# Summing three groups of the modulation product on VectorE instead of TensorE

## What is computed

```python
sc, scc = jax.nn.silu(c), jax.nn.silu(c_ctx)
mod_l = sc @ ada_w[i] + ada_b[i]                     # 6 * 1024 values: sh1, s1, g1, sh2, s2, g2
mod_c = scc @ ada_w[i] + ada_b[i]
h = x * (1 + s1) + sh1
x = layernorm(ALPHA * x + g1 * mixer(h), ln1_g[i], ln1_b[i])
x = layernorm(ALPHA * x + g2 * mlp(x * (1 + s2) + sh2), ln2_g[i], ln2_b[i])
```

## Time and profile before

| what | value |
|---|---|
| median of 3 runs | 1933.3 us (1932.83 to 1934.34) |
| the profiled execution's own time | 1933.96 us |
| its span in the profile | 1932.1 us |
| TensorE matmuls busy | 1921.8 us, 99% |
| VectorE busy | 1371.3 us, 71% |
| ScalarE busy | 674.7 us, 35% |
| GpSimd busy | 381.2 us, 20% |
| mean granted TensorE clock | 0.999 |

### The profile page before, as it was taken

The page is one execution under the profiler, slowest core; times in us unless marked ns, Lnnn a source line. Parts: engine busy times, 40 slices in busy tenths (PEclk is TensorE's granted clock), DMA queues, the critical chain, the costliest instruction groups (busy, mean ns, idle before and its releaser), DMA issues.

```text
span 1932.1 us, 24878 instructions
## 1 busy us (share of the span) xinstructions
PE 1921.8 (99%) x9432; PEld 1653.0 (86%) x9432; DVE 1371.3 (71%) x1977; ACT 674.7 (35%) x936; POOL 381.2 (20%) x364
## 2 busy tenths in 40 slices
PE   9999999999999999999999999999999999999998
PEld 6889899899889988998888888888888888888887
DVE  3756587698887777767887755754764787777778
ACT  2423122145323222331546225324413443434443
POOL 0300312313211222222310130130030037110004
PEclk9999999999999999999999999999999999999999
DMA  9623334345998998898596285366447525977656
GB/s 327 262 70 67 120 121 131 106 135 134 210 230 216 215 230 231 229 236 226 175 223 240 88 251 181 129 192 197 151 144 231 173 90 178 246 210 194 175 146 148
DMA packets 120419, 350.59 MB, mean 181 GB/s; under 512 B 17520, under 2 KB 30448, under 8 KB 115568
## 3 DMA queue, kind: packets, MB, share of 16 engines
q1 hardware_dynamic: 91200, 268.11, 40.9%
q0 software_dynamic: 27280, 77.08, 22.2%
q10 hardware_dynamic: 1824, 3.85, 0.6%
HBM read 296.01 MB, written 40.92 MB: 174 GB/s over the span
## 4 chain that ended last, share of the span: by engine, by line
PE 95%; POOL 1%; DMA 1%; DVE 1%; issue 1%; ACT 0%; SPq 0%; POOLq 0%; DVEq 0%; ACTq 0%
PE bank L1157 18%; PE bank L1159 18%; PE bank L1158 18%; PE bank L1195 4%; PE bank L1196 4%; PE bank L1197 4%; PE bank L1565 3%; PE bank L1564 3%; PE bank L1562 3%; PE bank L1626 3%; PE bank L1627 3%; PE bank L1624 3%; PE bank L1809 2%; PE bank L1808 2%; PE bank L1806 2%; PE bank L1468 1%
## 5 line engine op out<-in xcount | busy, mean ns | idle before, releaser
L2377 DVE TENSOR_TENSOR w_lo<-raw,w_hi 128x1024 fp32r<-128x1024 f32 x132 | 168.8, 1282 | 170.8 <-ACT w_hi L1832 170.6
L1832 ACT ACTIVATE w_hi<-raw 128x1024 fp32r<-128x1024 f32 x132 | 139.2, 1055 | 279.3 <-PE bank L1159 158.9
L1157 PE MATMUL bank<-w_hi,act_hi 128*128 128x512 f32 x504 | 198.2, 393 | 0.0
L1159 PE MATMUL bank<-w_hi,act_lo 128*128 128x512 f32 x504 | 196.4, 390 | 0.0
L1158 PE MATMUL bank<-w_lo,act_hi 128*128 128x512 f32 x504 | 196.3, 390 | 0.0
L1157 PE MATMUL bank<-hT_hi,w_hi 128*128 128x384 f32 (+2 forms) x544 | 191.8, 353 | 0.0
L1158 PE MATMUL bank<-hT_lo,w_hi 128*128 128x384 f32 (+2 forms) x544 | 190.8, 351 | 0.0
L1159 PE MATMUL bank<-hT_hi,w_lo 128*128 128x384 f32 (+2 forms) x544 | 190.8, 351 | 0.0
L1195 PE MATMUL bank<-w_hi,hT_hi 128*128 128x512 f32 x336 | 131.0, 390 | 0.0
L1196 PE MATMUL bank<-w_lo,hT_hi 128*128 128x512 f32 x336 | 130.8, 389 | 0.0
L1197 PE MATMUL bank<-w_hi,hT_lo 128*128 128x512 f32 x336 | 130.7, 389 | 0.0
(11 more groups left out here) (458 smaller groups left out, 4858.2 us busy)
## 6 DMA issues: line engine op xcount, KB each, us to landing
raw<-w_units_d SPq DMA_DIRECT2D x234, 512.0 KB, 4.6
mod<-mod_units_d SPq DMA_DIRECT2D x64, 384.0 KB, 4.5
wsum<-w_units_d SPq DMA_DIRECT2D x44, 512.0 KB, 4.5
raw<-weight_sums_d SPq DMA_DIRECT2D x32, 512.0 KB, 4.4
wsum<-w_units_d POOLq DMA_DIRECT2D x25, 512.0 KB, 7.9
wsum<-wsum POOLq DMA_DIRECT2D x19, 512.0 KB, 7.0
bv<-mod_units_d SPq DMA_DIRECT2D x16, 512.0 KB, 3.6
weight_sums_d<-w_units_d POOLq DMA_DIRECT2D x8, 1024.0 KB, 12.4
```

The source lines that it names most:

```text
L1157: nc.tensor.matmul(out, s_hi, m_hi, start=first, stop=False)
L1159: return nc.tensor.matmul(out, s_lo, m_hi, start=False, stop=last)
L1832: nc.scalar.activation(halves_of(phase, k, i)[0], raw[:, s, :], ACT.Copy).then_inc(hi_done, 1)
L2377: tt(lo, raw[:, s, :], f32(hi), ALU.subtract).then_inc(lo_done, 1)
```

## The change

The sum over partitions of the three groups moves to VectorE. It transposes each accumulated tile of 128 x 1024 in blocks of 32 x 32 and sums each block's 32 columns (`part_sum`), which leaves, in each band of 32 partitions, the sums over that band's rows, 32 columns for each vector. Four matmuls (`part_columns`) then add the four bands: the stationary tile `sel32` is 128 x 32, with a one where the partition's number modulo 32 is the column's, and each matmul takes 8 x 2 of the partial sums as moving columns and writes one band of bank 7. VectorE adds the bias (`add_part_bias`). `sel32` is made by one row sum of the identity. The row sums' matmuls, ScalarE's copies and the transposes of the three groups go. In vz VectorE's sums stand between the low halves of units 1 and 2, and the matmuls after unit 2. In the two gmlp trips VectorE's sums stand between the last two low halves of the down stage, the matmuls after token tile 1 of the last sweep, and the bias addition behind the drain of that tile. The semaphore `lg_dve` is renamed `small_done` and also counts `sel32` and the sums. The fourth group, in gmlpz, and the second layer keep the old way.

```diff
@@ order of TensorE's steps
-_VZ = _V[:2] + [("rows2", 6, "A")] + _V[2:3] + [("cols2", 7, "D")] + _V[3:]
+_VZ = _V[:3] + [("cols2", 7, "D")] + _V[3:]
...
-_DOWN0M = _DOWN0[:1] + _ROWS + _COLS + _DOWN0[1:]
+_DOWN0M = _DOWN0[:10] + _COLS + _DOWN0[10:]
@@ buffers and counts
+        part_sums = bst[:, :, :, :].rearrange("p a b c -> p (a b c)")[:, 0:64].rearrange("p (v n) -> p v n", v=2)
+        sel32 = sb("sel32", [P, 32])
...
+        part_sums_v = rbuf[:, 0, 0:64].rearrange("p (v n) -> p v n", v=2)
...
+        def sums_made(phase, i):
+
+            done = 11
+            if phase == "vz":
+                return done
+            return done + 4 * (i + 1)
@@ TensorE
-                            if columns:
-                                columns()
...
-                                    if t == 1 and columns1:
+                                    if t == 1 and half == 1 and columns1:
                                         columns1()
...
-                                if half == 0 and rows:
-                                    rows()
...
+            def part_columns(phase, i, label, n, vectors):
+                sums = part_sums_v if phase == "vz" else part_sums
+
+                pe.wait_ge(small_done, sums_made(phase, i))
+                free(phase, i, label)
+                for q in range(4):
+                    src = sums[:, 0:vectors, 0:4 * n].rearrange("p v (j q) -> p q j v", q=4)[:, q]
+                    last = nc.tensor.matmul(bank[7][32 * q:32 * q + 32, 0:n * vectors].rearrange("p (j v) -> p j v", v=vectors),
+                                            sel32[:, :], src, start=True, stop=True, tile_position=(0, 32 * q))
+                last.then_inc(pe_step, 1)
...
-            def sums_2():
-                pe.wait_ge(mod0_used, KC)
-                mod_sums("vz", 0, "rows2", 6, sums_v, WIDE_M0 // 2)
-
             for phase, i in V_PIECES:
                 token_units(phase, i, 0, "v", TILES0, {} if phase == "v" else {
-                    (1, 5): sums_2, (2, 5): lambda: mod_columns("vz", 0, 2, rbuf[:, 0, :], 7)})
+                    (2, 5): lambda: part_columns(phase, i, "cols2", 8, 2)})
...
                 elif phase != "gmlpz":
-                    down(phase, i, CH, TILES0, act_hi0, act_lo0, ready, rows=rows, columns=columns)
+                    down(phase, i, CH, TILES0, act_hi0, act_lo0, ready,
+                         columns1=lambda: part_columns(phase, i, "cols0", 8, 2))
@@ ScalarE
                 if phase == "vz":
-                    mod_rows(phase, i, 2, rbuf[:, 0, :], 6, step_of("v0", 0, "cols3"))
+                    act.wait_ge(mod0_used, KC)
...
-                    down_splits(phase, i, CH, copy if p else None)
+                    down_splits(phase, i, CH, None)
@@ VectorE
-            def down(phase, i, k0, tiles, then=None):
+            def down(phase, i, k0, tiles, then=None, sums=None, columns=None):
...
                 split_lo(phase, i, k0 + 3)
+                if sums:
+                    sums()
                 if phase == "ffn1a":
                     block_lo(0, 0)
                 else:
                     split_lo(phase, i, k0 + 4)
                 for t in range(tiles):
                     drain(phase, i, 1, t, tiles)
+                    if t == 1 and columns:
+                        columns()
...
+            def part_sum(done, v, a, src, turned, sums=part_sums):
+
+                n = src.shape[1] // 32
+                dve.wait_ge(small_done, done)
+                nc.vector.transpose(turned, src).then_inc(small_done, 1)
+                dve.wait_ge(small_done, done + 1)
+                nc.vector.tensor_reduce(sums[:, v, a:a + n], turned.rearrange("p (n r) -> p n r", r=32),
+                                        mybir.AxisListType.X, ALU.add).then_inc(small_done, 1)
+
+            def add_part_bias(phase, i, label, layer, c, n, vectors):
+
+                dve.wait_ge(pe_step, step_of(phase, i, label))
+                src = bank[7][:, 0:n * vectors].rearrange("p (j v) -> p j v", v=vectors)
+                bias = cols[:, ADAB + 48 * layer + c:ADAB + 48 * layer + c + n].unsqueeze(2).to_broadcast([P, n, 2])
+                tt(modc[:, layer, c:c + n, :], src, bias, ALU.add).then_inc(dve_drain, 1)
...
-                    dve.wait_ge(pe_step, step_of("gmlp", m // KC - 1, "cols0"))
+                    dve.wait_ge(small_done, sums_made("gmlp", m // KC - 1))
...
                 split_lo(phase, i, 1)
                 if n < 2:
                     product_v(4 * n)
+                if n == 2:
+                    dve.wait_ge(mod0_used, KC)
+                    for v in range(2):
+                        part_sum(7 + 2 * v, v, 0, sums_v[v], stage[:, :, :].rearrange("p a b -> p (a b)"), part_sums_v)
                 split_lo(phase, i, 2)
...
+                    nc.vector.tensor_reduce(sel32[:, :], ident[:, :].rearrange("p (x r) -> p r x", x=4), mybir.AxisListType.X,
+                                            ALU.add).then_inc(small_done, 1)
                 split_lo(phase, i, 4)
                 if n < 2:
                     product_v(4 * n + 3)
                 else:
-                    mod0_columns(phase, i, "cols2", 7, 2)
+                    add_part_bias(phase, i, "cols2", 0, 8 * 2, 8, 2)
...
                 if phase != "gmlpz":
-                    def then():
-                        normalise_v(p + 1)
-                        if p:
-                            mod0_columns(phase, i, "cols0", 7, 2 + p)
-                    down(phase, i, CH, TILES0, then)
+                    def group_sums():
+                        dve.wait_ge(mod0_used, KC * (p + 1))
+                        for v in range(2):
+                            part_sum(sums_made(phase, i) - 4 + 2 * v, v, 0, sums_g[v], stage[:, :, :].rearrange("p a b -> p (a b)"))
+
+                    def group_columns():
+                        add_part_bias(phase, i, "cols0", 0, 8 * (2 + p), 8, 2)
+                    if p:
+                        down(phase, i, CH, TILES0, lambda: normalise_v(p + 1), group_sums, group_columns)
+                    else:
+                        down(phase, i, CH, TILES0, lambda: normalise_v(p + 1))
```

More of the change, by code:

```diff
@@ L523, in build @@
         lgh_ready = sem("lgh_ready")
-        lg_dve = sem("lg_dve")
+        small_done = sem("small_done")
         lg_act = sem("lg_act")
@@ L1202, in token_units, with down @@
                             between[q, t]()
-            def down(phase, i, k0, tiles, a_hi, a_lo, ready, late=None, rows=None, columns=None, rows1=None, columns1=None):
+            def down(phase, i, k0, tiles, a_hi, a_lo, ready, late=None, rows1=None, columns1=None):
                 for half in range(2):
@@ L2081, in _ @@
                 if n == 0:
-                    act.wait_ge(lg_dve, 1)
+                    act.wait_ge(small_done, 1)
                     nc.scalar.activation(lg[:, 3, :], lg[:, 2, :], ACT.Ln).then_inc(lg_act, 1)
@@ L2952, in _ @@
                     dve.wait_ge(lg_act, 1)
[L2953 to L2961, removed]
+                    ts(lg[:, 2, :], lg[:, 1, :], -1.0, 1.0, ALU.mult, ALU.add).then_inc(small_done, 1)
+                    dve.wait_ge(small_done, 1)
+                    ts(lg[:, 4, :], lg[:, 2, :], -1.0, 1.0, ALU.mult, ALU.add).then_inc(small_done, 1)
+                    dve.wait_ge(small_done, 2)
+                    ts(lg[:, 4, :], lg[:, 4, :], 1e-30, None, ALU.max).then_inc(small_done, 1)
+                    dve.wait_ge(small_done, 3)
+                    nc.vector.reciprocal(lg[:, 4, :], lg[:, 4, :]).then_inc(small_done, 1)
+                    dve.wait_ge(small_done, 4)
+                    tt(lg[:, 0, :], lg[:, 4, :], lg[:, 1, :], ALU.mult).then_inc(small_done, 1)
                 for t in range(TILES0):
@@ L2968, in _ @@
                 if n == 0:
[L2969 removed]
+                    dve.wait_ge(small_done, 5)
                     dve.wait_ge(lg_act, 2)
[L2971 removed]
+                    tt(lg[:, 0, :], lg[:, 0, :], lg[:, 3, :], ALU.mult).then_inc(small_done, 1)
+                    nc.vector.tensor_reduce(sel32[:, :], ident[:, :].rearrange("p (x r) -> p r x", x=4), mybir.AxisListType.X,
+                                            ALU.add).then_inc(small_done, 1)
                 split_lo(phase, i, 4)
@@ L3199, in _ @@
             dve.wait_ge(dec_in, 32)
-            dve.wait_ge(lg_dve, 6)
+            dve.wait_ge(small_done, 6)
             first_k = first
```

## The result

The changed kernel takes 1946.03 us (median of 6 runs, 1945.14 to 1947.62) against 1933.07 for the kernel before (6 runs): **1.0066 times as long, 95% interval 1.0053 to 1.0079**. It was forecast at 1929.5, at most 1932.9. It came out 13.0 us slower than before and 16.5 us above the forecast. The profiled execution took 1945.8 us, its span 1944.0.

A forecast was written before the change was run, and what follows sets the result against it. TensorE was taken as the bound; 3 x 1.20 (row sums) + 3 x 0.45 (transposes) - 3 x 0.38 (added matmuls) = 3.8 us saved takes the median from 1933.3 to 1929.5 us, range 1928.8 to 1932.9.

The forecast's parts named there:

- What bounds the kernel: Whole kernel: TensorE, busy 99% of the span, so its time removed in the edited places should reach the end.
- Removed 1.65 us a group, added 0.38: TensorE, three groups: row-sum matmuls (1.20 us) and transposes (0.45) go, four narrow matmuls come; net 1.27 us per group.
- The extrapolation over columns: Narrow matmuls: a line through the costs at 512 and 384 columns gives 0.38 us for 16 columns.
- VectorE's instructions at 1.25 us: Two transposes and two row sums per group at 1.25 us each, 5.2 us with waits, between 3.2 and 8.4.
- No stretch beside GpSimd: In gmlp, GpSimd's residual additions would not lengthen the new VectorE instructions; a 0.39 us stretch would use up the spare.
- The room in gmlp, 5.6 us for 5.2: In the edited gmlp down stages VectorE's four instructions fit before TensorE's wait, with 0.4 us to spare.
- The selection matrix is one small row sum: Making sel32 on VectorE takes one small row sum, lying before a 0.80 us wait.
- A: VectorE's transposes pass at half rate; TensorE waits 2.1 us twice in gmlp, giving 1933.7 us; chance 0.13.
- B: The added narrow matmuls cost their full loads, 0.89 us a group, giving 1931.0 us; chance 0.10.
- C: VectorE's transposes and row sums both at half rate; TensorE waits 9.2 us in two pieces; 1938.7 us, slower; chance 0.06.
- D: The time saved on TensorE is lost at the next wait and nothing moves, 1933.3 us; chance 0.04.
- Gaps outside the edited places: The forecast's test: it is wrong if TensorE's gaps grow anywhere outside the named places; no size given.

The follow-up runs named there:

- experiment 2: Changed kernel with sel32 kept in 32 unused columns of layer 1's modulation tile instead of its own tile: 1929.82 us, ratio 0.998.
- experiment 3: Changed kernel with sel32 in the first half of a 256-byte tile instead of a 128-byte one: 1929.49 us, ratio 0.9979.
- experiment 1: Kernel before with an unused tile of 128 bytes a partition where the changed kernel puts sel32: 1949.72 us, ratio 1.0084.
- experiment 8: experiment 2 with each gmlp transpose done twice, the second overwriting the first with the same values: 1934.90 us, ratio 1.0006.
- experiment 6: Kernel before with 128 unused bytes just ahead of w_hi, moving the split weights and all later tiles: 1951.25 us, ratio 1.0092.

## Why the prediction was wrong, point by point

- **What bounds the kernel: right.** TensorE was and is the bound, and its time in the edited places reaches the end: 3 x 1.27 predicted, 3.6 and 3.9 us measured (experiments 2 and 3, where the tiles keep their distances or shift by 256 bytes).
- **Removed 1.65 us a group, added 0.38: right.** The narrow matmuls measured 0.40, the net gain 1.26. The extrapolation over columns was the better choice than the full loads of the earlier trace rows.
- **VectorE's instructions at 1.25 us: right.** Transposes 1.23 to 1.25, row sums 1.22, four of them 5.0 us with their waits. The Trainium skill's "Vector Engine (DVE) Microarchitecture Reference", section 3.8 (one element per cycle per lane), fits: with 1.24 us for 1024 columns the transpose takes as long as the row sum and the two-input instructions of that size, and not twice as long. The figure of "VectorE: DVE Perf Modes", section "The three transpose paths", 311 ns for 128x128 in bf16, would have made it an estimated 2.5; the measurement decides against carrying it over to this fp32 form.
- **No stretch beside GpSimd: right.** GpSimd adds residuals until 288.83 in the changed kernel, over the whole of the first transpose (287.60), which took 1.23 us; the two-input subtraction just ahead of it took 1.62. That agrees with the rule of the Trainium skill's "SBUF — State Buffer", section "Who interferes with whom", that the prediction weighed.
- **The room in gmlp, 5.6 us for 5.2: right, and narrow.** In experiment 2 the last row sum ends at 292.77 + 1.22 = 293.99, and the narrow matmuls are due one spacing after 294.50, at 294.73: 0.7 us to spare. VectorE's slack at gmlpz's first chunk is 0.93 us there (1.04 in the earlier trace rows), so its lag was absorbed.
- **"The selection matrix is one small row sum": the step that failed.** It priced the instruction and left out the tile. The sum 3 x 1.20 + 3 x 0.45 - 3 x 0.38 has no term for it, and gives no reason why placement should cost nothing. The diff's `sb("sel32", [P, 32])` is an edit with a cost of its own: 128 bytes that slide the operands of some 3,400 matmuls against each other, 16.3 us by experiment 1, and 16.2 by the changed kernel against experiment 2. No row of the trace before could price it, which was a reason to name it as unknown and widen the range upward.
- **Rivals A, B and C: none happened.** C had the right sign, from a mechanism that played no part. D is out too, since 3.6 us were gained. None of the four asked what the change does on the side. Their prices rest on "every microsecond that VectorE is late for a TensorE wait costs one", which is too low: in the profile of experiment 8 a wait of 1.73 us cost 3.43.
- **Gaps outside the edited places**: the prediction named them as what would prove it wrong. It was wrong without any gap: TensorE stayed 99% busy and each matmul took longer. The test should have been the spacing of an untouched matmul.

Two versions beat both kernels: experiment 2 (1929.82 us) and experiment 3 (1929.49 us), each by 0.2%, the gain that was forecast. Their intervals overlap; there is nothing to choose between them by time.

## What to carry to other kernels

A new SBUF tile is an edit to every tile that is placed after it. Put it last, or into a tile that exists, or round its size up to a multiple that was measured to be free (256 bytes here, where it restores the cost of the kernel before; no run tells whether another placement would be faster still), and compare the mean duration of untouched matmuls in both profiles before looking for waits. Where TensorE is the bound, a wait on it can cost more than its length: here up to twice, when its clock fell behind it.

## What the runs showed of the hardware that I had not expected

**A shift of a matmul's two operands against each other in a partition changes its spacing.** For products of split fp32 (fp32r) with 512 moving columns and a 128x128 stationary tile, start to start is 0.227 us at the distance of the kernel before, 0.233 at 32 and at 64 bytes from it, 0.232 at 128 and 0.229 at 192 (19 matmuls in a row in a down stage); with 384 columns the mean duration goes from 334 to 338 ns at 128 bytes. A displacement of 256 bytes leaves both unchanged, and moving both operands by 128 bytes does too. Why, stays open. That the moving operand's reads meet the loading of the next matmul's weights is a guess that no run tests, and the exact distances at which the cost begins and ends were not tried.

**A pause of 1.7 to 2.1 us on TensorE was followed by a fall of its clock.** Both pauses in the profile of experiment 8 were followed by about 3 us at 0.43 us a matmul, and the first cost 3.43 us instead of 1.73. TensorE had been busy without a break for over 200 us before it (busy 234.00 us of 234.00 from 56 to 290). The profile of experiment 6 has a third case, in a place that no edit touches, and that of experiment 2 a shorter pause there:
```profile
923.29 0.45 PE L1563 MATMUL bank<-hT_hi,w_hi 128*128 128x384 f32 x1 [2.09 <-DVE w_lo L2509]
```
```profile
913.82 0.44 PE L1577 MATMUL bank<-hT_hi,w_hi 128*128 128x384 f32 x1 [0.91 <-DVE w_lo L2523]
```
After the 2.09 us the granted clock was 1.00 until 924, 0.50 from 925 to 927, and 1.00 again from 928 on. From 920.87 to 928.11 it took 7.24 us for 19 spacings that take 3.33 at 0.1755 each: 3.9 us lost, most of what sets the profiled execution of experiment 6 (1955.24 us) apart from its other three (1950.48 to 1951.92). After the 0.91 us it stayed at 1.00.
